# Hybrid encoder layer on eight cores: the PSUM banks of the mixer's score pairs and of its other TensorE work put into one pool of five

## The chip, the cores and the metric

The kernel runs on the 8 cores of one Trainium2 chip. Every core takes one sequence of the batch of 8 (2048 tokens by 1024 features) through the whole layer; the cores exchange nothing. The metric is the device time of the slowest core, in microseconds (us). TensorE (PE) multiplies, ScalarE (ACT) and VectorE (DVE) take results out of PSUM, GpSimd (POOL) computes small columns and issues the weight loads, SyncE (SP) issues the other transfers. PSUM has 8 banks, numbered 0 to 7 here, each 128 partitions by 512 fp32.

## The reference

```python
mod = (jax.nn.silu(c) @ w_ada[l] + b_ada[l]).reshape(bsz, N_MOD, D_MODEL)
x = sandwich(x, swiglu FFN 1,  ..., 0.5)      # D_FF = 2816
x = sandwich(x, hybrid_mixer,  ..., 1.0)
x = sandwich(x, swiglu FFN 2,  ..., 0.5)
def sandwich(x, y_fn, g_pre, g_post, shift, scale, gate, weight):
    h = rms_norm(x, g_pre) * (1.0 + scale[:, None, :]) + shift[:, None, :]
    y = rms_norm(y_fn(h), g_post)
    return x + weight * gate[:, None, :] * y
def hybrid_mixer(...):                        # chunks of 64 tokens
    proj = h @ w_in + b_in                    # qa ka va qb kb vb, 2304 columns
    oa = band attention, 8 heads on 2 kv heads, own + 2 chunks back, ALiBi, sinks
    ob = band attention, 8 heads, own + 8 chunks back, relative-position bias
    return concat(rms_norm(oa), rms_norm(ob)) @ w_out + b_out
```

The attention of both groups is a plain softmax over a band of keys: scores, exponential, product with V, division by the sum. All weights are used in bf16, sums are fp32.

## The kernel before

A core works its sequence in two halves of 1024 tokens, each of 8 tiles of 128 tokens (`m` = 0 to 7). For each half the program runs gate/up of the first FFN (lines 635 and 638), its down product (666 and 676), the mixer, gate/up of the second FFN and its down product. In the second half the mixer's first tiles also see keys of the first half, so that it has 56 score pairs against 45 in the first.

Every instruction is recorded by `S.op` into the queue of one engine, with the keys that it reads and writes; a PSUM bank is one such key. At run time each engine takes its queue in strict order, and an instruction waits until the keys that it needs are free. The order of the queues is decided while the program is built. The recorder also keeps a small model of time (`S.t`, `S.avail`, the `cost` arguments), and the mixer's main loop asks it, each time round, which of the candidate pieces of PE work could start first.

The pieces of PE work of a mixer are these. In the rows of the order and of the profile each is known by its lines.

- **Score pair** (`s_pair`, lines 878 with 882 or 888): scores of one key tile for two sets of four heads, into two banks. The bias is put in first by a product with the identity (878). Then ACT takes both banks out as two exponentials into `PT` (line 894). At most 8 units (4 pairs) may be pending ahead of their products with V.
- **PV unit** (`pv_unit`, line 916, 4 small matmuls): one exponential times V, summed in banks 2, 3 and 4. Two belong to a pair.
- **Fillers**: projections of the half's second four tiles (`proj_T` line 711, 13 pieces; `proj_VA` line 740 and `proj_V` line 725, four each), and 40 pieces of gate/up of the second FFN (`gu_chunk` line 787). Gate/up pieces may start only when the tail of tile 3 is done, since they read the new HT of tiles 0 to 3. A gate piece is taken out by ACT (Tanh, 793) and then DVE (795), an up piece by DVE (799).
- **Tail of a tile**, a chain of 13 steps across the engines: group norm of the attention's result (ACT 943, POOL 484 and 486, DVE 955), transposes (PE 966, DVE 970), output projection in two halves of 8+1 matmuls (PE 981 and 983), square and gate of each half (ACT 574, DVE 580), the residual (DVE 592), the next norm (ACT 495, DVE 502), and transposes into HT (`back2`, PE 524, ACT 509 and DVE 512).

Before the change the banks are in three groups. Score pairs rotate over banks 0, 1 and 5. PV sums live in 2, 3 and 4. Everything else, fillers and tails, uses 6 and 7:

```python
SBANKS = (0, 1, 5)
sb_ = [SBANKS[(u + r) % 3] for r in range(2)]
cbanks = [6, 7]
```

Output half `hh` always takes bank 6 + hh, and while it waits for its gate the bank is in the set `hold`, so that no filler takes it; with both held no filler is a candidate. The last transposes of a tail take 6 and 7 together. When all score pairs and PV units are recorded (`late`), fillers get banks 0 to 5 instead. The weight loads are recorded when a filler has released its ring slot, one megabyte each, three slots, in a fixed order.

Of the kernel before, what the change touches and what calls it, by code (L numbers as in the profile page):

```python
# [164 lines left out]
def build_nc(stage=3, dbg=False):  # L165
# [96 lines left out]
    S = Sched()  # L262
# [253 lines left out]
    def back(s, t, xb, bank, split=True):  # L516
        src, skeys = XBUF[xb]
        where = lambda k: (bank + 1, (k - 4) * 128) if split and k >= 4 else (bank, k * 128)
# [8 lines left out]
        S.op('pe', fn, reads=skeys + [("identb",)], writes=[ps_key(bank)] + ([ps_key(bank + 1)] if split else []), cost=0.46)  # L527
        for k in range(8):
            bk, c0 = where(k)
            mod_evac(s, k, HT[:, k, t * 128:(t + 1) * 128], PSB[:, bk, c0:c0 + 128], ps_key(bk),  # L530
                     [("HT", t, k)], bk != bank)
# [153 lines left out]
    def mixer(hf):  # L685
# [91 lines left out]
        cbanks = [6, 7]  # L777

# [59 lines left out]
        SBANKS = (0, 1, 5)  # L838
# [13 lines left out]

        def s_deps(u):
# [3 lines left out]
            return kk[0 if kind == "A" else 1] + qk, [ps_key(SBANKS[(u + r) % 3]) for r in range(2)]  # L857
# [10 lines left out]
        def s_pair(u):  # L868
# [4 lines left out]
            sb_ = [SBANKS[(u + r) % 3] for r in range(2)]  # L873
# [102 lines left out]
        def tail_b(m, hh):  # L976
            hold.add(6 + hh)

            def fn2(e):
                for k in range(8):  # L980
                    e.matmul(PS[6 + hh][:], lhsT=HT[:, k, m * 128:(m + 1) * 128], rhs=WOUT[:, hh, k, :],  # L981
                             start=(k == 0), stop=False)
                return e.matmul(PS[6 + hh][:], lhsT=ONES[:, :], rhs=BHL[:, 640 + hh * 512:640 + (hh + 1) * 512],
                                start=False, stop=True)
            S.op('pe', fn2, reads=[("wo", hh)] + [("HT", m, k) for k in range(8)] + [("ones",), ("bhi",), ("blo",)],
                 writes=[ps_key(6 + hh)], regions=("R1hi",), cost=1.94)

        def back2(m):
            back(2, m, m % 2, 6)

        chains = {}
        hold = set()
# [3 lines left out]

        def first_free(banks):
            return min(banks, key=lambda b: S.avail('pe', [], [ps_key(b)]))

        def chain(m):  # L1000
# [4 lines left out]
            bb = [ps_key(6), ps_key(7)]  # L1005
            ta = lambda: first_free([b for b in (6, 7) if b not in hold])

            def sq(hh):
                if hh == 0:
                    v["c"] = newst(2)  # L1010
                half_square(6 + hh, v["c"] + hh)
                if hh == 1:
                    v["p"] = None

            def gate(hh):
                half_gate(m, hh, 6 + hh, v["c"] + hh)
                hold.discard(6 + hh)
                if hh == 1:
                    v["p"] = half_root(v["c"])

            def fsq():
                v["f"] = front_square(X[:, m, :], fx)
            chains[m] = [
                ('act', lambda: (xh, [("sg", 0)]), lambda: o_norm(m, v), ()),
                ('dve', lambda: (stk(), [("yb", 0), ("yb", 1)]), lambda: o_scale(m, v), ()),
                ('pe', lambda: ([("yb", 0), ("yb", 1)], [ps_key(ta())]), lambda: tail_a(m, ta()), None),
                ('pe', lambda: ([("HT", m, 0)], bb[0:1]), lambda: tail_b(m, 0), (6,)),
                ('pe', lambda: ([("HT", m, 0)], bb[1:2]), lambda: tail_b(m, 1), (7,)),
                ('act', lambda: (bb[0:1], [("sg", 0)]), lambda: sq(0), ()),
                ('dve', lambda: (bb[0:1] + [("st", v["c"])], xh), lambda: gate(0), ()),  # L1030
                ('act', lambda: (bb[1:2], [("sg", 0)]), lambda: sq(1), ()),
                ('dve', lambda: (bb[1:2] + [("st", v["c"] + 1)], xh), lambda: gate(1), ()),
                ('dve', lambda: ([("st", v["p"])] + xh, fx), lambda: post_add(m, False, hf, v["p"]), ()),
                ('act', lambda: (fx, [("sg", 0)]), fsq, ()),
                ('dve', lambda: ([("st", v["f"])], xh), lambda: front_scale(X[:, m, :], fx, m % 2, v["f"]), ()),
                ('pe', lambda: (xh, bb), lambda: back2(m), (6, 7))]
# [312 lines left out]
```

## Time and profile before

| | |
|---|---|
| three runs | 1364.27, 1365.14, 1462.91 us, median 1365.14 |
| the profiled execution | 1369.62 us, of which 1367.7 us lie between its first and last instruction |
| spans of the 8 cores | 1358.3 to 1367.7 us, the profiled one is the longest |
| PE busy | 1285.5 us, 94% of the span |
| ACT, DVE, POOL busy | 447.7, 457.3, 188.1 us |
| scheduled part of the mixer, first half | about 336 to 543 us |
| scheduled part of the mixer, second half | about 972 to 1199 us |

A busy time says how long an engine had an instruction at work. What is left of a window is idle, and for PE that is what this document is about. The granted clock is a share of TensorE's full speed: 1.00 is the level of 2.4 GHz, and a window that was partly at 1.2 GHz has a figure between. A row of the timeline has the start, the duration, the engine, the line, what is written from what, and in brackets the idle time before it with what ended it.

### The profile page before, as it was taken

How to read it: one execution, taken by the hardware profiler on the slowest of the kernel's cores; microseconds unless marked ns; L12 is line 12 of the kernel's file. 1: busy time of each engine (PE TensorE's matmuls, PEld its weight loads, DVE VectorE, ACT ScalarE, POOL GpSimd, SP SyncE). 2: the span in 40 equal slices, each digit the busy share in tenths (PEclk: the TensorE clock that was granted, in tenths of full speed). 3: DMA queues.
4: the chain of work that ended last, by engine and by line, in shares of the span. 5: the costliest groups of instructions: out<-in, count | busy, mean ns of one | idle time of the engine just before them, and what ended most of it. 6: DMA issues, size and time to landing. Idle time of an engine off the chain costs nothing.

```text
span 1367.7 us, 21754 instructions; the slowest of 8 cores (1358.3 to 1367.7 us)
## 1 busy us (share of the span) xinstructions
PE 1285.5 (94%) x7941; PEld 611.2 (45%) x7941; DVE 457.3 (33%) x835; ACT 447.7 (33%) x902; POOL 188.1 (14%) x394
## 2 busy tenths in 40 slices
PE   2799999999989999999999999999998799999997
PEld 1344444554444444444444444444444344444443
DVE  2131122452454454222442122243143445522122
ACT  2241111342656552212341111233465655221110
POOL 3011101120121112101220000111011111200000
PEclk9999999999999999999999999999999999999999
DMA  9998977658243339993558756203542034899111
GB/s 174 173 201 144 169 130 125 113 88 158 47 85 73 69 69 163 169 156 122 170 144 156 126 101 113 38 0 65 91 84 41 2 63 92 146 162 159 43 47 61
DMA packets 32095, 148.24 MB, mean 108 GB/s; under 512 B 3274, under 2 KB 8567, under 8 KB 20344
## 3 DMA queue, kind: packets, MB, share of 16 engines
q0 software_dynamic: 26128, 129.64, 54.1%
q1 hardware_dynamic: 5864, 17.22, 3.5%
q8 instruction: 65, 1.06, 0.3%
q14 instruction: 38, 0.31, 0.1%
HBM read 258.36 MB, written 8.40 MB: 195 GB/s over the span
## 4 chain that ended last, share of the span: by engine, by line
PE 87%; DMA 4%; ACT 3%; DVE 2%; issue 2%; POOL 0%; DVEq 0%; ACTq 0%; POOLq 0%
PE psall L676 21%; PE psall L635 17%; PE psall L638 17%; PE psall L787 10%; PE psall L711 6%; PE psall L981 4%; DMA RING<-w_gu 3%; PE psall L878 3%; PE psall L725 2%; PE psall L916 2%; PE psall L888 1%; PE psall L666 1%; DMA R<-w_ada 1%; PE psall L524 1%; ACT R L894 1%
## 5 line engine op out<-in xcount | busy, mean ns | idle before, releaser
L676 PE MATMUL psall<-R 128*128 128x512 bf16 x1320 | 288.7, 379 | 0.0
L635 PE MATMUL psall<-HT,RING 128*128 128x512 bf16 x928 | 221.5, 382 | 6.0 <-DMA RING<-w_gu 4.9
L645 DVE TENSOR_TENSOR R<-SG,psall 128x512 bf16<-128x512 f32 x136 | 93.4, 687 | 381.3 <-ACT SG L643 357.7
L638 PE MATMUL psall<-HT,RING 128*128 128x512 bf16 x928 | 220.5, 381 | 0.0
L643 ACT ACTIVATE SG<-psall 128x512 f32<-128x512 f32 x136 | 81.2, 597 | 375.9 <-PE psall L638 375.7
L676 PEld LDWEIGHTS psall<-R 128*128 128x128 bf16 x1320 | 128.4, 98 | 151.2
L787 PE MATMUL psall<-HT,RING 128*128 128x512 bf16 x640 | 151.1, 387 | 4.2 <-ACT HT L509 2.4
L635 PEld LDWEIGHTS psall<-HT,RING 128*128 128x128 bf16 x928 | 90.7, 98 | 115.9 <-issue 10.8
L638 PEld LDWEIGHTS psall<-HT,RING 128*128 128x128 bf16 x928 | 91.2, 98 | 110.7 <-issue 3.1
L894 ACT ACTIVATE R<-psall 128x512 bf16<-128x512 f32 x202 | 109.7, 597 | 66.9 <-PE psall L888 50.9
L711 PE MATMUL psall<-HT,RING 128*128 128x512 bf16 x416 | 95.2, 380 | 0.2 <-ACT HT L509 0.2
L560 ACT ACTIVATE SG<-psall 128x1024 bf16<-128x1024 f32 x32 | 32.8, 1024 | 188.7 <-PE psall L676 188.7
L787 PEld LDWEIGHTS psall<-HT,RING 128*128 128x128 bf16 x640 | 60.0, 99 | 75.0 <-issue 18.9
L484 POOL TENSOR_SCALAR ST<-ST 128x1 f32<-128x1 f32 (+1 forms) x108 | 26.3, 244 | 419.8 <-ACT SG L560 184.2
L568 DVE TENSOR_TENSOR XH<-psall,GG 128x1024 f32<-128x1024 f32 x32 | 39.1, 1222 | 133.3 <-ACT SG L560 133.3
L509 ACT ACTIVATE HT<-psall,COLA,GMOD 128x128 bf16<-128x128 bf16 (+1 forms) x180 | 68.7, 464 | 23.3 <-DVE COLA L442 15.3
L285 POOL DMA_DIRECT2D RING<-w_gu x53 | 30.9, 586 | 317.7 <-PE psall L638 225.5
L486 POOL TENSOR_TENSOR ST<-ST,NHALF 128x1 f32<-128x1 f32 (+1 forms) x108 | 69.3, 641 | 16.7 <-POOL ST L484 1.3
L592 DVE SCALAR_TENSOR_TENSOR X<-XH,ST,X 128x1024 f32<-128x1024 f32 x48 | 61.6, 1284 | 10.5 <-DVE XH L568 5.1
L981 PE MATMUL psall<-R,HT 128*128 128x512 bf16 x256 | 61.0, 381 | 0.4 <-DVE HT L970 0.4
L711 PEld LDWEIGHTS psall<-HT,RING 128*128 128x128 bf16 x416 | 38.5, 98 | 45.6 <-issue 2.6
L495 ACT ACTIVATE SG<-X 128x1024 bf16<-128x1024 f32 x40 | 42.2, 1056 | 50.4 <-DVE X L592 48.6
(131 smaller groups left out, 1062.8 us busy)
## 6 DMA issues: line engine op xcount, KB each, us to landing
RING<-w_gu POOLq DMA_DIRECT2D x53, 1024.0 KB, 9.8
R<-w_down POOLq DMA_DIRECT2D x44, 512.0 KB, 17.3
R<-w_ada POOLq DMA_DIRECT2D x10, 1024.0 KB, 20.5
RING<-w_in POOLq DMA_DIRECT2D x10, 1024.0 KB, 9.9
RING<-w_ada POOLq DMA_DIRECT2D x8, 1024.0 KB, 9.8
out<-X SPq DMA_DIRECT2D x16, 512.0 KB, 2.6
R<-w_gu POOLq DMA_DIRECT2D x5, 1024.0 KB, 54.0
X<-x POOLq DMA_DIRECT2D x8, 512.0 KB, 27.2
```

The lines of the kernel that those rows point to most:

```text
L486: S.op('pool', lambda e: e.tensor_tensor(out=ST[:, c3:c3 + n], in0=ST[:, c3:c3 + n], in1=NHALF[:, 0:n], op=ALU.pow), reads=k1 + [("nhalf", ...
L509: S.op('act', lambda e: e.activation(out=dst, in_=psrc, func=AF.Identity, bias=sh, scale=GMOD[:, s, k:k + 1]), reads=rd, writes=wkeys, cos ...
L592: S.op('dve', lambda e: e.scalar_tensor_tensor(out=X[:, t, :], in0=XH[:, xb, :], scalar=ST[:, c3:c3 + 1], in1=X[:, t, :], op0=ALU.mult, op ...
L635: e.matmul(PS[bG][:], lhsT=rb[:, k, jj * 128:(jj + 1) * 128], rhs=HT[:, k, tb * 512:(tb + 1) * 512], start=(k == 0), stop=(k == 7))
L638: ins = e.matmul(PS[bU][:], lhsT=rb[:, k, 256 + jj * 128:256 + (jj + 1) * 128], rhs=HT[:, k, tb * 512:(tb + 1) * 512], start=(k == 0), sto ...
L643: S.op('act', (lambda e, bG=bG, sgi=sgi: e.activation(out=SG[:, sgi, :], in_=PS[bG][:], func=AF.Silu)), reads=[ps_key(bG)], writes=[("sg", ...
L645: S.op('dve', (lambda e, bU=bU, sgi=sgi, j=j, tb=tb: e.tensor_tensor(out=AT[:, tb, j, :], in0=SG[:, sgi, :], in1=PS[bU][:], op=ALU.mult)), ...
L676: ins = e.matmul(PS[bk][:], lhsT=AT[:, t // 4, j, (t % 4) * 128:(t % 4 + 1) * 128], rhs=WD[:, j, hh * 512:(hh + 1) * 512], start=(j == 0), ...
L711: ins = e.matmul(PS[bank][:], lhsT=RING[:, slot, k, g * 128:(g + 1) * 128], rhs=HT[:, k, tb * 512:(tb + 1) * 512], start=(k == 0), stop=(k ...
L787: ins = e.matmul(PS[bank][:], lhsT=RING[:, slot, k, part * 256 + jj * 128:part * 256 + (jj + 1) * 128], rhs=HT[:, k, 0:512], start=(k == 0 ...
L894: S.op('act', (lambda e, r=r, pi=pi: e.activation(out=PT[pi], in_=PS[sb_[r]][:], func=AF.Exp, scale=0.125)), reads=[banks[r]], writes=[("p ...
L981: e.matmul(PS[6 + hh][:], lhsT=HT[:, k, m * 128:(m + 1) * 128], rhs=WOUT[:, hh, k, :], start=(k == 0), stop=False)
```

## The change

`SBANKS` and `cbanks` go. There is one list, `pool = [0, 1, 5, 6, 7]`. A score pair takes the two banks of the pool that the model of time says are free first and that are not in `hold`. A filler, the first transposes of a tail and each output half take the one that is free first; an output half keeps the bank that it got in `v["b", hh]` until its gate is recorded. The last transposes take the two free first. A step that needs a bank for an output half is not a candidate while two banks are held, but fillers no longer stop then. When `late` comes, banks 2, 3 and 4 join the pool (in all 8 banks against 6 before). No instruction is added or taken away; the order and the banks are new.

```diff
-        SBANKS = (0, 1, 5)
+        pool = [0, 1, 5, 6, 7]
+        hold = set()
+        def two_free():
+            return sorted([b for b in pool if b not in hold], key=lambda b: S.avail('pe', [], [ps_key(b)]))[:2]
+        def first_free():
+            return two_free()[0]
...
-            return kk[0 if kind == "A" else 1] + qk, [ps_key(SBANKS[(u + r) % 3]) for r in range(2)]
+            return kk[0 if kind == "A" else 1] + qk, [ps_key(b) for b in two_free()]
...
-        def tail_b(m, hh):
-            hold.add(6 + hh)
+        def tail_b(m, hh, bank):
+            hold.add(bank)
...
-            back(2, m, m % 2, 6)
+            back(2, m, m % 2, two_free())
...
-            if len(hold) == 2 if need is None else any(b in hold for b in need):
+            if len(hold) >= 2 and need:
                 return False
...
-            fn(first_free(free_banks()))
+            fn(first_free())
...
-                cbanks[:] = [0, 1, 5, 2, 3, 4]
+                pool[:] = [0, 1, 5, 2, 3, 4, 6, 7]
```

The rows below are in the order in which PE takes them, equal rows merged with a count. 128x512 x2 of the identity is the start of a score pair, 128x65 are PV units of four matmuls each. The changed file has its lines about seven further down: 878 is 885 there, 882 is 889, 888 is 895, 916 is 923, 711 is 712, 725 is 726, 740 is 741, 787 is 786, 966 is 973, 981 is 988, 524 is 525.

**Place 1.** PE at the start of the first half's scheduled part, before:

```order
L878 MATMUL psall<-EA,IDENTB 128x512 x2
L882 MATMUL psall<-R 128x512 x2
L711 MATMUL psall<-HT,RING 128x512 x8
L916 MATMUL psall<-R 128x65 x8
L878 MATMUL psall<-EB,IDENTB 128x512 x2
L888 MATMUL psall<-R 128x128 x8
L711 MATMUL psall<-HT,RING 128x512 x8
```

and with the change:

```order
L885 MATMUL psall<-EA,IDENTB 128x512 x2
L889 MATMUL psall<-R 128x512 x2
L885 MATMUL psall<-EB,IDENTB 128x512 x2
L895 MATMUL psall<-R 128x128 x8
L712 MATMUL psall<-HT,RING 128x512 x8
L923 MATMUL psall<-R 128x65 x16
```

A filler stood after every pair; now it stands after every second, and the PV units follow two pairs behind their scores.

**Place 2.** PE in the second half, from the last projection piece to the first gate/up piece, where only pairs and tails are left. Before, there are 16 pairs in it, of which the first two stand here:

```order
L725 MATMUL psall<-RING,HT 128x512 x8
L727 MATMUL psall<-BHL,ONES 128x512
L916 MATMUL psall<-R 128x65 x8
L878 MATMUL psall<-EA,IDENTB 128x512 x2
L882 MATMUL psall<-R 128x512 x2
L916 MATMUL psall<-R 128x65 x4
L524 MATMUL psall<-IDENTB,XH 128x128 x8
L916 MATMUL psall<-R 128x65 x4
L878 MATMUL psall<-EB,IDENTB 128x512 x2
L888 MATMUL psall<-R,KBP 128x128 x8
L916 MATMUL psall<-VBP,R 128x65 x4
L966 MATMUL psall<-IDENTB,YB 128x128 x8
```

and with the change there are 9, of which the first two stand here:

```order
L726 MATMUL psall<-RING,HT 128x512 x8
L728 MATMUL psall<-BHL,ONES 128x512
L988 MATMUL psall<-R,HT 128x512 x8
L990 MATMUL psall<-BHL,ONES 128x512
L988 MATMUL psall<-R,HT 128x512 x8
L990 MATMUL psall<-BHL,ONES 128x512
L923 MATMUL psall<-R 128x65 x8
L885 MATMUL psall<-EB,IDENTB 128x512 x2
L895 MATMUL psall<-R 128x128 x8
L885 MATMUL psall<-EB,IDENTB 128x512 x2
L895 MATMUL psall<-R 128x128 x8
L923 MATMUL psall<-R 128x65 x4
```

The last projection piece stood behind pair 22 of the half's 56; now it stands behind pair 32. The first gate/up piece stood behind pair 38; now it stands behind pair 41.

**Place 3.** PE in the first half, where the four small projections (740) meet the output projection of a tile, before:

```order
L981 MATMUL psall<-R,HT 128x512 x8
L983 MATMUL psall<-BHL,ONES 128x512
L916 MATMUL psall<-R 128x65 x12
L740 MATMUL psall<-RING,HT 128x128 x8
L742 MATMUL psall<-BHL,ONES 128x128
L740 MATMUL psall<-RING,HT 128x128 x8
L742 MATMUL psall<-BHL,ONES 128x128
L740 MATMUL psall<-RING,HT 128x128 x8
```

and with the change:

```order
L988 MATMUL psall<-R,HT 128x512 x8
L990 MATMUL psall<-BHL,ONES 128x512
L923 MATMUL psall<-R 128x65 x16
L712 MATMUL psall<-HT,RING 128x512 x32
L741 MATMUL psall<-RING,HT 128x128 x8
L743 MATMUL psall<-BHL,ONES 128x128
L741 MATMUL psall<-RING,HT 128x128 x8
```

Four large projections (712) now stand between the output projection and the small ones.

## Rows read from the trace of the kernel before

**Rows 1.** The page: busy times of the engines, and the chain that ended last by engine.

```profile
PE 1285.5 (94%) x7941; PEld 611.2 (45%) x7941; DVE 457.3 (33%) x835; ACT 447.7 (33%) x902; POOL 188.1 (14%) x394
...
PE 87%; DMA 4%; ACT 3%; DVE 2%; issue 2%; POOL 0%; DVEq 0%; ACTq 0%; POOLq 0%
```

**Rows 2.** Windows of core 7: length, busy of PE, PEld, DVE, ACT, POOL, clock, DMA.

```profile
336.00:543.00 207.00, 197.81 (x1491) 94.73 (x1489) 101.25 (x209) 109.39 (x234) 34.25 (x76) 0.97 0.47 83
400.00:410.00 10.00, 9.46 (x47) 4.49 (x47) 3.84 (x8) 3.41 (x6) 2.43 (x5) 0.73 0.56 106
972.00:1199.00 227.00, 209.91 (x1680) 101.68 (x1680) 101.47 (x210) 120.51 (x256) 34.18 (x76) 0.98 0.39 69
1040.00:1086.00 46.00, 33.22 (x338) 16.84 (x337) 20.29 (x49) 30.73 (x71) 8.12 (x19) 0.93 0.13 24
1040.00:1050.00 10.00, 7.29 (x68) 4.05 (x67) 4.59 (x12) 6.46 (x16) 2.71 (x5) 0.68 0.56 105
```

**Rows 3.** Groups of instructions by line, PE, 1040 to 1086 us.

```profile
L878 PE MATMUL psall<-EB,IDENTB 128*128 128x512 bf16 x22 | 7.4, 423 | 0.0
...
L878 PE MATMUL psall<-EA,IDENTB 128*128 128x512 bf16 x10 | 3.0, 379 | 0.0
```

**Rows 4.** Groups of instructions by line, ACT, 1040 to 1086 us.

```profile
L894 ACT ACTIVATE R<-psall 128x512 bf16<-128x512 f32 x32 | 17.3, 596 | 8.5 <-PE psall L888 6.7 <-PE psall L882 1.7
```

**Rows 5.** Waits of PE, 1040 to 1086 us: total, times, longest.

```profile
PE psall L916 <- ACT R L894: 8.9, 10, 1.9
PE psall L787 <- ACT HT L509: 1.6, 1, 1.6
```

**Rows 6.** Timeline of PE, pairs without a filler.

```profile
1075.02 0.40 PE L888 MATMUL psall<-R 64*128 64x128 bf16 x8
1076.26 0.28 PE L916 MATMUL psall<-R 128*128 128x65 bf16 x4 [0.84 <-ACT R L894]
1076.38 0.59 PE L878 MATMUL psall<-EB,IDENTB 128*128 128x512 bf16 x2
...
1077.23 0.30 PE L916 MATMUL psall<-R 128*128 128x65 bf16 x4
```

**Rows 7.** Timeline of ACT, the same place.

```profile
1075.52 1.08 ACT L894 ACTIVATE R<-psall 128x512 bf16<-128x512 f32 x2 [0.27 <-PE psall L888]
1077.40 1.08 ACT L894 ACTIVATE R<-psall 128x512 bf16<-128x512 f32 x2 [0.80 <-PE psall L888]
1078.37 1.06 ACT L495 ACTIVATE SG<-X 128x1024 bf16<-128x1024 f32 x1
```

**Rows 8.** Waits of PE, 336 to 543 us.

```profile
PE psall L740 <- DVE XH L580: 2.6, 1, 2.6
PE psall L916 <- ACT R L894: 2.5, 9, 0.4
PE psall L878 <- ACT R L696: 1.0, 1, 1.0
```

**Rows 9.** Timeline of PE, first half, around the small projections.

```profile
398.98 1.01 PE L740 MATMUL psall<-RING,HT 128*128 128x128 bf16 x8 [2.58 <-DVE XH L580]
...
401.55 3.62 PE L725 MATMUL psall<-RING,HT 128*128 128x512 bf16 x8
...
406.69 1.90 PE L725 MATMUL psall<-RING,HT 128*128 128x512 bf16 x8
```

**Rows 10.** Timeline of DVE, the two gates that free the banks of one tile.

```profile
394.61 0.69 DVE L580 TENSOR_TENSOR XH<-psall,GG 128x512 f32<-128x512 f32 x1 [3.27 <-ACT SG L574]
...
398.15 0.68 DVE L580 TENSOR_TENSOR XH<-psall,GG 128x512 f32<-128x512 f32 x1
```

**Rows 11.** Timeline of all engines, a gate piece and what takes it out.

```profile
1090.62 1.89 PE L787 MATMUL psall<-HT,RING 128*128 128x512 bf16 x8
...
1092.61 0.60 ACT L793 ACTIVATE SG<-psall 128x512 f32<-128x512 f32 x1 [1.19 <-PE psall L787]
1093.37 0.69 DVE L795 SCALAR_TENSOR_TENSOR SG<-SG,psall 128x512 f32<-128x512 f32 x1 [1.26 <-ACT SG L793]
```

## What the change will do: the prediction

> **What bounds the kernel now.** I read the busy times first. PE is at work for 1285.5 of 1367.7 us, and 87% of the chain that ended last is PE's own work [rows 1]. The other engines are busy for a third of the span. So PE is the bound, no PE instruction is taken away, and the change can win only what PE idles, or runs at the low clock, inside the two scheduled parts of the mixer. Outside of them nothing is edited.
>
> Then I read the windows of these two parts [rows 2]. In the first half PE is busy 197.81 of 207 us, so it idles 9.2. In the second it is busy 209.91 of 227, so it idles 17.1. Together 26.3 us, 1.9% of the time. Of the 17.1 us, 46 - 33.22 = 12.8 lie in one stretch, 1040 to 1086 us. That stretch is the one where all projections are used up and the gate/up pieces are not allowed yet. The reader is to see there 32 products with the identity [rows 3], so 16 pairs, 2.9 us each, and 32 exponentials [rows 4].
>
> Why PE idles there is in the waits: 8.9 us in ten waits of PV units for ACT's exponentials, and 1.6 us for the first gate/up piece, which waits for the HT of tile 3 [rows 5]. But ACT is not full either, 30.73 of 46 us [rows 2]. The timelines show the loop. A pair's last score products end at 1075.42; the two exponentials run from 1075.52; the first PV unit starts at 1076.26, after 0.84 us idle, and the next pair right behind it at 1076.38 [rows 6]. Its exponentials start at 1077.40, and ACT idled 0.80 us before them [rows 7]. Each engine waits for the other: with three banks, of which a pair takes two, the next pair needs a bank of the pair before. The period is 77.40 - 75.52 = 1.88 us, of which ACT has 1.08 for two exponentials.
>
> **The thin stretch, with the change (Places 1 and 2).** It acts twice. Five banks let a second pair stand between PE and ACT, so the loop opens: in Place 2 two pairs stand back to back and PV units follow a pair or two behind. And since pairs run ahead where fillers are, fillers last longer: 9 pairs are left uncovered and not 16.
>
> What would the nine cost? PE's own work in the stretch is 33.22 us for 16 pairs with their tails, 2.08 a pair, ACT's is 30.73 / 16 = 1.92 a pair [rows 2]. So even when the loop is open the two engines are nearly level, and a little idle time must stay. Low end: none but the 1.6 us for HT, which is a true dependence on tile 3. High end: the same idle rate as before, 12.8 x 9/16 = 7.2 us. I take 4, nearer to the low end, since the loop of rows 6 and 7 is what the extra banks break. **Gain 8.8 us** (5.6 to 11.2).
>
> **The rest of the second half.** 17.1 - 12.8 = 4.3 us of idle time in 181 us, in single waits of under a microsecond or so. The one at the start, a score pair that waits for the evacuation of a projection (the first half has the same, 1.0 us [rows 8]), stays: the first banks taken are again 0 and 1. **Gain 2 us** (0 to 3.3).
>
> **The first half.** 9.2 us idle. One wait is 2.6 us [rows 8]: a small projection needs bank 7, which holds an output half until DVE has gated it. DVE's queue had the division of the next tile between the two gates of this one, so that the second ran 3.5 us after the first, from 398.15 to 398.83 [rows 10], and PE went on at 398.98 [rows 9]. With the change this projection takes any free bank of three, and four large projections stand ahead of it (Place 3). It goes. Another 2.5 us are nine waits of PV units for exponentials [rows 8], of which the deeper queue takes most. 1.0 us at the start stays. The other 3.1 us are single waits on HT and on gates. I take 2.6 + 2.0 + 0.9 = 5.5. **Gain 5.5 us** (2.6, the one wait alone, to 8.2, all but the start).
>
> **The clock.** Behind both stretches the granted clock falls: 0.73 from 400 to 410 us and 0.68 from 1040 to 1050 [rows 2]. Before the first fall stood the 2.6 us wait; the second fell while PE idled for exponentials. The price is in the durations: the projection at 401.55 took 3.62 us against 1.90 for the same one at 406.69 [rows 9], 1.7 us. Of the 1.01 us of the small one at 398.98, at the same ratio, 0.5 is the clock's, and its neighbour's is alike, so the first fall cost about 2.5 us; the second, of like depth and length, is taken as 2.4. They need not go with their waits, and new ones may come. **Gain 2.5 us**, half of the 4.9 (0 to 4.9).
>
> The Trainium skill (TensorE: Matmul & The Clock Gate, "Why this matters for your kernels") says that idle gaps between bursts of matmuls bring TensorE back to its lower clock. By it both falls would go with the gaps, and this term would be the whole 4.9. The trace agrees that both falls lie in idle stretches. But the whole stretch has 0.93 in the mean and its first ten us 0.68, so the other 36 us ran at (46 x 0.93 - 6.8) / 36 = 1.00 although PE idled in them as well [rows 2]. Idle time and clock don't go together closely, and I keep the half.
>
> **What is added.** No instruction, transfer or byte. POOL's queue keeps its loads in the same ring order. Seven fewer pairs behind the last projection means that the loads released by projections are issued later in the half, yet nine pairs and an output projection, over 20 us, still stand between the last projection and the first gate/up piece; I cost the loads at nothing. The cover is that distance; without it a late load would show as a wait of line 786 on the ring. What is added is **coupling**: a score pair can now be given a bank whose last user was a gate/up piece, and behind a waiting pair stand all of PE's queue and ACT's exponentials. A gate piece that ended on PE at 1092.51 was taken by ACT at 1092.61 and by DVE from 1093.37 to 1094.06 [rows 11], so its bank is free 1.6 us after its end, and an exponential's bank 0.7 to 1.2 us after the pair's [rows 6, 7]. In the new order three banks are used per cycle of a pair, two PV units and a filler, about 3 us, so a bank comes back after 5/3 of a cycle, 5 us. That covers it where the model of time is right. Where it is wrong, PE waits. Below: 0. Above: a wait of 0.8 us, like that of rows 6, in every seventh of the about 85 cycles with a filler (61 fillers a half less the 19 or so behind the last pair, twice), 10 us. **Cost 4 us**, nearer the low end because the 5 us are three times the 1.6.
>
> **Sum.** 8.8 + 2 + 5.5 + 2.5 - 4 = 14.8 us. The profiled execution had 1369.6, so 1354.8. The median of the runs, 1365.1, is 4.5 us under that execution, so the forecast is **1350 us**, 1.1% faster. Of this kernel a change of under 2%, 27 us, can't be told from none here.
>
> **Rivals.**
>
> *The banks were not the limit.* PE and ACT are level in the thin stretch (2.08 against 1.92 us a pair), so breaking the loop could give nothing there: PE then waits for ACT in longer pieces. For it: the tails put another 13 us of ACT work between the exponentials (30.73 - 17.3) [rows 2, 4], and a pair's exponentials can stand behind them; only moving seven pairs under cover is left, and the new waits eat that. Against it: ACT idled 0.80 us before a pair that was next in its queue [rows 7]. Gain then the 2.6 us wait and about 1 more: 1361.5 us. Chance 0.23. In the Trainium skill (TensorE: Matmul & The Clock Gate, "HAM oscillation") double-buffering PSUM gave a kernel no further gain once its loop was in order; by that the time would be this rival's, or none at all.
>
> *All the waits go.* Idle 26.3 less 1.0 at each start and 1.6 for HT is 22.7, and 4.9 of clock: 27.6 us, 1337.5 at the edge of 2%. For it: nothing but loops and banks stands in the waits of rows 5 and 8. Against it: near level engines. Chance of 1342 or less 0.09, of more than 2% 0.03.
>
> *Slower, by coupled banks.* The mechanism of the last term, not rare but regular: in the stretches with gate/up pieces every pair meets a bank whose gate piece still waits behind a tail's work in DVE's queue. One division kept the second gate 3.5 us behind the first [rows 10]. Before, only fillers met that. If in each of the 85 cycles a pair waited 0.6 us, it would cost 51 us against 18.8 gained, 1397 us. It decides from 18.8 / 85 = 0.22 us a cycle upward, and is over 2% from 0.54. Against it: the 5 us of distance, three times the release. Chance of slower at all 0.07, of over 2% slower 0.02.
>
> **Chances and range.** Forecast (1342 to 1358) 0.61; banks not the limit (1358 to 1366) 0.23; all the waits 0.09; slower 0.07. The range 1341 to 1364 leaves out about 0.07 below and 0.12 above. Faster by over 2%: 0.03; within 2%: 0.94; slower: 0.03.
>
> **What would show it.** In the second half the stretch between the last projection and the first gate/up piece should be under 25 us with 18 exponentials, ACT over 80% busy in it, and PE's waits of PV units for exponentials 3 us or less over the half, against 8.9 in the stretch alone. In the first half the wait of the small projection on DVE's gate should be gone, and the total idle time of the first part about 4 us, of the second about 7. Coupling would show as waits of score pairs (now line 885) on DVE's or ACT's evacuation of gate/up pieces, above 4 us together. I would be wrong if the first gate/up piece waits long for HT, because tile 3's tail, now behind more exponentials in ACT's queue, ends later than the pairs run out, or if a clock fall moves into the projections.

## The result, and the profile after

| | before | after |
|---|---|---|
| median of the runs, us | 1364.99 | 1339.32 |
| profiled execution, us | 1369.62 | 1339.02 |
| its longest span, us | 1367.7 | 1337.5 |

The ratio of the times is 0.9816, with an interval of 0.9803 to 0.9829. The change makes the kernel 1.8% faster, 25.7 us: inside the 2% bound, but clear of no change by its interval. The forecast was 1350 us in a range of 1341 to 1364, so the gain was larger than forecast and the time lies just under the range. A later comparison gave 0.9827 (0.9814 to 0.984). Some executions, of most kernels here, are longer at a lower clock on the four cores of one die or on all eight (1591.43 us once, of the changed kernel); the ratios and intervals leave them out, the medians don't.

In the profiled executions the cores 0 to 3 had mean clocks of 0.989 to 0.998, and their median span is 1360.9 us before and 1334.7 us after, 26.2 us less. So the gain doesn't rest on cores 4 to 7, whose clock was lower in the profile before (0.987 to 0.990).

First the page of the changed kernel: the span, the busy times, and the chain that ended last by engine.

```profile
span 1337.5 us, 21760 instructions; the slowest of 8 cores (1332.2 to 1337.5 us)
...
PE 1272.5 (95%) x7941; PEld 606.3 (45%) x7941; DVE 456.9 (34%) x835; ACT 445.2 (33%) x902; POOL 188.0 (14%) x394
...
PE 91%; DMA 4%; ACT 1%; issue 1%; DVE 1%; POOL 0%; DVEq 0%; ACTq 0%; another core or an unknown queue 0%; POOLq 0%
```

PE is busy for 13.0 us less than before with the same 7941 matmuls [rows 1]. So the gain is not idle time alone. The rows that follow are those of core 0, the slowest, where no other core is named. The windows of the two scheduled parts, which now end earlier, and of the thin stretch in the second half (columns as in rows 2):

```profile
332.00:532.00 200.00, 195.96 (x1512) 94.90 (x1510) 103.57 (x213) 109.13 (x235) 34.32 (x76) 1.00 0.49 89
960.00:1169.00 209.00, 203.48 (x1680) 99.33 (x1680) 101.99 (x211) 119.51 (x256) 34.22 (x76) 1.00 0.42 75
1044.00:1062.00 18.00, 15.86 (x185) 8.06 (x183) 7.88 (x20) 13.99 (x32) 3.30 (x8) 1.00 0.31 60
```

PE idles 4.0 us in the first part (9.2 before) and 5.5 in the second (17.1 before). The clock is 1.00 in all three windows, where it was 0.97, 0.98 and 0.93 [rows 2]. The thin stretch has 9 pairs in 18 us, 2.0 a pair, against 16 in 46 us, 2.9 a pair. PE is at work for 88% of it and ACT for 78% (the prediction had said over 80%). From the first output projection at 1044.28 to the first gate/up piece at 1061.61 it is 17.3 us, under the 25 of the prediction. PE's waits (total, times, longest), in the first half,

```profile
PE psall L885 <- ACT R L697: 1.0, 1, 1.0
PE psall L636 <- DVE R L798: 0.9, 1, 0.9
...
PE psall L923 <- ACT R L901: 0.6, 2, 0.3
```

and in the second:

```profile
PE psall L525 <- ACT R L901: 1.6, 1, 1.6
PE psall L885 <- ACT R L697: 1.0, 1, 1.0
PE psall L636 <- DVE R L798: 0.9, 1, 0.9
...
PE psall L923 <- ACT R L901: 0.3, 1, 0.3
```

The ten waits of PV units for exponentials in the thin stretch, 8.9 us [rows 5], are gone; of this kind 0.3 us is left. So is the 2.6 us wait of the small projection for a gate [rows 8]. No score pair waits for the evacuation of a gate/up piece, on any core. The 1.0 us in each half at line 885 is the first pair, as before. The one wait that answers to the coupling that the prediction feared is the 1.6 us of line 525. Behind the last pair of a half the pool has eight banks, six before; PE idles 1.2 us there before and 1.6 after, so these two banks are no part of the gain.

One sign that the prediction had named did show, on some cores: gate/up pieces that wait for their weights. Core 4 of the same execution:

```profile
PE psall L786 <- DMA RING<-w_gu: 1.4, 1, 1.4
```

Cores 2 and 7 have 0.4 and 0.9 us of it, and in the later profile of the same kernel four cores have 0.4 to 1.7 us. Before, no core has such a wait in the two parts.

The timeline of PE in the thin stretch, core 0 again, shows the wait of line 525 and the open loop:

```profile
1051.16 0.42 PE L923 MATMUL psall<-R 128*128 128x65 bf16 x8
1051.41 0.59 PE L885 MATMUL psall<-EA,IDENTB 128*128 128x512 bf16 x2
1051.94 0.39 PE L889 MATMUL psall<-R 64*128 64x512 bf16 x2
1052.26 0.42 PE L923 MATMUL psall<-R 128*128 128x65 bf16 x8
1052.52 0.59 PE L885 MATMUL psall<-EA,IDENTB 128*128 128x512 bf16 x2
...
1058.18 0.61 PE L525 MATMUL psall<-IDENTB,XH 128*128 128x128 bf16 x8 [1.55 <-ACT R L901]
```

From one pair (1051.41) to the next (1052.52) it is 1.11 us, against 1.88 in rows 6 and 7, and eight PV matmuls stand between without a wait. At 1058.18 the last transposes of tile 3 had to wait for a bank whose exponential stood in ACT's queue. ACT in the same place:

```profile
1049.44 3.04 ACT L901 ACTIVATE R<-psall 128x512 bf16<-128x512 f32 x6 [0.27 <-PE psall L895]
...
1053.36 2.10 ACT L901 ACTIVATE R<-psall 128x512 bf16<-128x512 f32 x4
...
1057.35 2.04 ACT L901 ACTIVATE R<-psall 128x512 bf16<-128x512 f32 x4
```

Six exponentials run back to back in 3.04 us, where ACT idled 0.80 us before a pair of them [rows 7]. The exponential for which line 525 waited is the first at 1057.35; it had the two group norms of the next tile (950, not shown, 1055.85 to 1057.45) ahead of it in ACT's queue.

I timed the stages on all cores from the timelines. A half is counted from the first `proj_V` to the first gate/up product behind the mixer; what lies between the halves is 398.6 us in both kernels and behind the second half 168.4 us.

| core of the profiled execution | first half, us (PE busy) | second half, us (PE busy) |
|---|---|---|
| before, core 7 (the slowest) | 236.0 (226.3) | 257.2 (239.0) |
| before, core 1 (fewest clock falls) | 233.3 (223.1) | 253.6 (234.3) |
| after, core 0 (the slowest) | 224.3 (220.1) | 238.4 (232.6) |
| after, core 1 | 224.1 (219.9) | 238.4 (232.6) |

Of core 7's 30.5 us, 9.7 + 18.2 - 4.2 - 5.8 = 17.9 are idle time and 12.6 are busy time. The busy part has three sources. The falls behind waits, at 400 and 1040 us, are in rows 2. Further falls stood in dense stretches late in the parts, on cores 4 to 7 alone; on core 7 they come to about 4.5 us, an estimate from the clocks of its 5 us windows. These are windows of core 7 and of core 1 of the kernel before, the same stretch, each counted from its core's own start:

```profile
515.00:525.00 10.00, 10.00 (x49) 4.66 (x48) 6.04 (x9) 1.20 (x2) 2.65 (x5) 0.89 1.04 172
```

```profile
515.00:525.00 10.00, 10.00 (x54) 4.81 (x53) 4.07 (x6) 1.54 (x4) 0.00 (x0) 1.00 1.01 163
```

PE was at work all the time on both, and only core 7 was at 0.89. And third, the end of a matmul's row is hidden only if another matmul follows at once. The four PV matmuls at 1076.26 have a row of 0.28 us, but the next row starts 0.12 us after them [rows 6]; ahead of a wait the whole row counts as busy. Core 1 has 49 places where PE ran out of work in the two halves before, and 20 after. It had one fall in the halves, of about 1.7 us by the windows, and has 4.9 us less busy time after. The other 3.2 us are put down to these row ends, 0.11 us for each of the 29 places; that is what is left over, and no run tests it. The profile models the ends of matmuls, so where busy time stops and idle time starts is its choice; the sum of both is not.

### The profile page after: what moved, and what is told of

Read it like the earlier page. It is cut to its first block, busy times and chain, and to the rows that moved or that the text cites. A ratio compares the mean times of both kernels' runs of the same rounds, so it can differ in the third digit from the quotient of the medians.

```text
span 1337.5 us, 21760 instructions; the slowest of 8 cores (1332.2 to 1337.5 us)
## 1 busy us (share of the span) xinstructions
PE 1272.5 (95%) x7941; PEld 606.3 (45%) x7941; DVE 456.9 (34%) x835; ACT 445.2 (33%) x902; POOL 188.0 (14%) x394
## 4 chain that ended last, share of the span: by engine, by line
PE 91%; DMA 4%; ACT 1%; issue 1%; DVE 1%; POOL 0%; DVEq 0%; ACTq 0%; another core or an unknown queue 0%; POOLq 0%
PE psall L677 21%; PE psall L636 17%; PE psall L639 17%; PE psall L786 10%; PE psall L712 6%; PE psall L988 4%; PE psall L885 3%; DMA RING<-w_gu 3%; PE psall L726 2%; PE psall L923 2%; PE psall L895 2%; PE psall L667 1%; DMA R<-w_ada 1%; PE psall L525 1%; PE psall L437 1%
## 5 line engine op out<-in xcount | busy, mean ns | idle before, releaser
L639 PE MATMUL psall<-HT,RING 128*128 128x512 bf16 x928 | 219.9, 380 | 0.0
L901 ACT ACTIVATE R<-psall 128x512 bf16<-128x512 f32 x202 | 107.1, 599 | 44.1 <-PE psall L895 30.6
L509 ACT ACTIVATE HT<-psall,COLA,GMOD 128x128 bf16<-128x128 bf16 (+1 forms) x180 | 68.7, 464 | 24.4 <-DVE COLA L442 15.7
```

Source lines behind the costliest of these rows:

```text
L509: S.op('act', lambda e: e.activation(out=dst, in_=psrc, func=AF.Identity, bias=sh, scale=GMOD[:, s, k:k + 1]), reads=rd, writes=wkeys, cos ...
L639: ins = e.matmul(PS[bU][:], lhsT=rb[:, k, 256 + jj * 128:256 + (jj + 1) * 128], rhs=HT[:, k, tb * 512:(tb + 1) * 512], start=(k == 0), sto ...
L901: S.op('act', (lambda e, r=r, pi=pi: e.activation(out=PT[pi], in_=PS[sb_[r]][:], func=AF.Exp, scale=0.125)), reads=[banks[r]], writes=[("p ...
```

## The experiments

All times below are medians unless said otherwise, all ratios are to the kernel before as run on the same chip beside it. Waits and timelines are of the slowest core of the profiled execution unless a core is named. Every kernel has line numbers of its own.

**Banks alone.** The decisions of the kernel before were written down (`SCRIPT`), and the changed kernel was made to follow them. In the traces of both, the instructions stand in the same order on PE, ACT, DVE and POOL.

```diff
+            want = script.pop(0)
+            go = [c for c in cand if c[3] == want][0]
-            now = S.t['pe'] + 0.1
-            go = min(cand, key=lambda c: (max(c[0], now), c[1]))
```

> Every engine's queue stands in the order of the kernel before, instruction by instruction; only the banks are those that the pool of five gives. Theory A (order and banks are worth something only together: in the old order a PV unit stands right behind the scores it needs, so a free bank doesn't help): only the 2.6 us wait of the small projection for a gate goes, with its clock fall, 2 to 6 us gained, about 1360 us; the waits of PV units for exponentials in the second half stay above 8 us. Theory B (the number of banks was the limit, the order only follows): most of the gain is here, 15 us or more, under 1350 us. Theory C (as in the prediction: the pool couples score pairs to slow evacuations): slower than the kernel before by up to 4 us.

Measured: 1362.27 us, ratio 0.9968 (0.9958 to 0.9978), 4 us of the 25. Waits of PE in the second half, and then in the first (926 is the PV unit, 904 the exponential, 976 the first transposes of a tail):

```profile
PE psall L926 <- ACT R L904: 11.7, 16, 1.9
```

```profile
PE psall L976 <- DVE YB L965: 3.0, 1, 3.0
PE psall L926 <- ACT R L904: 2.8, 10, 0.4
```

The waits for exponentials are all there (10.9 us in the same part of the kernel before). The small projection's wait is gone, but on this core a tail's first transposes wait 3.0 us in its place. Theory A holds in its time and in the waits that stay, but the clock fall near 400 us did not go: it is there on six of eight cores. Theories B and C fall: free banks with the old order win little, and they cost nothing. On core 1 the halves are 4.0 and 1.4 us shorter than before, 3.6 of it idle time.

**Order alone.** The order of the changed kernel (again the same on all four engines in the traces), the old groups of banks.

```diff
-            return sorted([b for b in pool if b not in hold], key=...)[:2]
+            return best([0, 1, 5])[:2]
...
-            return two_free()[0]
+            return best([b for b in (cbanks if late[0] else (6, 7)) if b not in hold] or [0, 1, 5])[0]
```

> Every engine's queue stands in the order of the changed kernel, but the banks are in the old groups: score pairs take two of 0, 1 and 5, everything else 6 and 7 (or, where both are held, one of 0, 1, 5). Theory A: two pairs back to back now need four banks and have three, so PE waits for exponentials at the second pair, about 0.9 us at each of some 30 such places; the gain of the fillers that are saved is eaten, 1350 to 1375 us. Theory D (saving fillers for the thin stretch is the whole gain): 1345 us or less. Theory B: no gain, 1365.

Measured: 1416.55 us, ratio 1.0376 (1.0358 to 1.0393). All three theories fell short here, A in size: the order without the banks loses 50 us. PE's waits, and the place where two pairs stand back to back (894 starts a pair, 910 is the exponential, 528 the last transposes of a tail, 801 what takes out an up piece):

```profile
PE psall L894 <- ACT R L910: 31.4, 32, 2.5
...
PE psall L528 <- DVE R L801: 6.5, 3, 3.1
```

```profile
348.83 0.60 PE L894 MATMUL psall<-EB,IDENTB 128*128 128x512 bf16 x2
349.36 0.40 PE L904 MATMUL psall<-R 64*128 64x128 bf16 x8
351.34 0.59 PE L894 MATMUL psall<-EB,IDENTB 128*128 128x512 bf16 x2 [1.58 <-ACT R L910]
```

The second pair waits 1.58 us for the exponentials of the first, since four banks are wanted and three are there. Such waits are 31.4 us; fillers and tails, which have two banks, wait as well. So the two halves of the change are worth -4 us and +50 us one by one, and -25 us together.

**Only the pairs get the pool.**

```diff
-            return ..., [ps_key(SBANKS[(u + r) % 3]) for r in range(2)]
+            return ..., [ps_key(b) for b in two_free()]      # of 0, 1, 5, 6, 7
```

> The kernel before, but score pairs may take any two of the five banks that are not held; fillers and tails stay on 6 and 7 and stop while both are held. 36 of the second half's 56 pairs stand ahead of the first gate/up piece with 1 pair in the thin stretch (16 before, 9 with the change). Theory A and D (running ahead saves fillers): nearly all of the gain, 1338 to 1346 us. Theory E (the freedom of fillers and tails matters as much, above all while output halves hold both banks): less than half of it, 1352 us or more.

Measured: 1390.89 us, ratio 1.018 (1.0163 to 1.0197), 24 us slower. I had expected nearly the whole gain. The pairs take banks 6 and 7, and fillers, which may use no other, starve: in the first half only 4 of the 13 large projections are placed before tile 3's pairs are done, and 9 stand in one lump, as tile 4 can't start without them. Waits of PE, and the timeline ahead of and in the lump (711, with a tail's transposes and output projection between):

```profile
PE psall L787 <- DMA RING<-w_gu: 10.2, 2, 5.6
...
PE psall L524 <- DVE XH L502: 6.4, 1, 6.4
```

```profile
390.33 0.61 PE L524 MATMUL psall<-IDENTB,XH 128*128 128x128 bf16 x8 [1.38 <-DVE XH L580]
392.29 5.30 PE L711 MATMUL psall<-HT,RING 128*128 128x512 bf16 x16 [1.36 <-DVE ST L933]
398.52 8.79 PE L711 MATMUL psall<-HT,RING 128*128 128x512 bf16 x39 [0.93 <-ACT R L696]
```

Pairs run uncovered, the tail's transposes wait up to 6.4 us for a norm, the lump's pieces wait for each other's evacuation on two banks, and the gate/up weights, whose loads wait for the projections to release the ring, are late by 10.2 us. The count of uncovered pairs between the last projection and the first gate/up piece (1 here) was a bad measure: the same hole had moved ahead of the lump.

**Only the fillers get the pool.**

```diff
-        cbanks = [6, 7]
+        cbanks = [0, 1, 5, 6, 7]
```

> The kernel before, but fillers may take any of the five banks; score pairs rotate over 0, 1, 5, tails stay on 6 and 7. Fillers go earlier: the last projection stands behind pair 13 in either half, with 14 and 25 pairs in the thin stretches (2 and 16 before). Theories A and D: slower, by 0.8 us for each of the 21 more uncovered pairs, 17 us, 1375 to 1390 us. Theory E: faster than before.

Measured: 1423.84 us, ratio 1.0421 (1.0404 to 1.0438). Theory E falls. The direction of A and D was right, the size over three times what 0.8 us a pair gives:

```profile
PE psall L916 <- ACT R L894: 20.2, 26, 2.0
PE psall L524 <- DVE XH L502: 16.3, 5, 7.1
PE psall L635 <- DMA RING<-w_gu: 13.9, 3, 5.0
```

Waits for exponentials are up from 13.4 us before, but the larger part is in waits that the estimate did not have, for norms, and for weights at the gate/up phase (13.9 us with the 5 of every run).

**Fixed banks for the tails.** Pairs and fillers share the five; a tail keeps 6 and 7.

```diff
-                v["b", hh] = first_free()
+                v["b", hh] = 6 + hh
...
-            back(2, m, m % 2, two_free())
+            back(2, m, m % 2, 6)
```

> The changed kernel, but a tail keeps banks 6 and 7 for its output halves and its last transposes, and one of them for its first transposes; pairs and fillers use all five. 13 pairs are uncovered in the second half (9 in the changed kernel). Theory L (pairs and fillers sharing a pool is what matters): within 5 us of the changed kernel, under 1345 us. Theory M (a tail that waits for just one bank, while pairs and fillers keep taking it, comes late, and with it the release of tile 3's HT and of the gate/up pieces): 10 us or more slower than the changed kernel, 1350 us or more, with waits of line 525 and 988.

Measured: 1351.06 us, ratio 0.9886 (0.9873 to 0.99), 8 us slower than the changed kernel in the same comparison (1342.91). Between the theories, nearer to M; waits of PE:

```profile
PE psall L786 <- DMA RING<-w_gu: 3.9, 1, 3.9
PE psall L525 <- DVE XH L581: 3.9, 2, 2.2
```

The last transposes wait 3.9 us for a gate on their fixed bank, and the gate/up pieces 3.9 us for weights. It is still 15.5 us faster than the kernel before beside it (1366.58), so pairs and fillers in one pool bring most of the gain, and the tails in it the rest.

**How deep a lead?** First at most two pairs ahead of their PV, then none.

```diff
-            if u < NU and len(pend) <= NPT - 2 and not blocked:
+            if u < NU and len(pend) <= 2 and not blocked:      # and, in the second, <= 0
```

> The changed kernel, but a score pair is a candidate only while at most one pair (two units) waits for its PV (four pairs before), so the lead of scores over PV is at most two pairs. Theory F (the loop is open as soon as one more pair stands between PE and ACT): within 4 us of the changed kernel, 1338 to 1343 us, ratio to the kernel before 0.980 to 0.984. Theory G (the deep lead matters, since it saves fillers and bridges ACT's tail work): a third or more of the gain is lost, 1348 us or more.

Measured: 1341.27 us, ratio 0.9829 (0.9812 to 0.9847), the same as the changed kernel's within the intervals. Theory F holds.

> The changed kernel, but a score pair is a candidate only when no PV unit waits, so that PE alternates between the scores of a pair and its own PV; 13 and 22 pairs are uncovered (1 and 9 in the changed kernel). Five banks are free to use. Theory F and G: the loop between PE and ACT is closed again and the thin stretch is longer than in the kernel before, about 1 us idle for each of 35 pairs, 1375 to 1395 us. Theory B (banks are the limit, the lead is not): within 5 us of the changed kernel.

Measured: 1381.75 us, ratio 1.0126 (1.011 to 1.0142). Waits of PE:

```profile
PE psall L923 <- ACT R L901: 19.5, 36, 1.0
```

With five banks and no lead the waits for exponentials are back, 36 of them. The lead is what the banks buy, and one pair more of it is enough. This kernel also leaves more pairs uncovered (22 against 9), so it doesn't part the lead from the fillers that it saves.

**Who chooses the bank?** The pool taken in turn.

```diff
+        turn = [0]
-            return sorted([b for b in pool if b not in hold], key=...)[:2]
+            return [b for b in pool[turn[0]:] + pool[:turn[0]] if b not in hold][:2]
+        def took(b):
+            turn[0] = (pool.index(b) + 1) % len(pool)
```

> The changed kernel, but the pool of five is taken in turn (held banks skipped) and not by the scheduler's choice of the bank free first. 5 pairs are uncovered in the second half. Theory H (coupling is harmless because five uses lie between two of one bank, whoever chooses): within 4 us of the changed kernel, 1337 to 1344 us. Theory I (the choice is what avoids the coupling: in turn, a score pair or a tail's transposes meet a bank whose evacuation is still queued on DVE): 8 us or more slower than the changed kernel, 1348 us or more, in waits of score pairs and transposes for DVE's and ACT's evacuation.

Measured: ratio 0.9897 (0.9845 to 0.9949). It is made of 1345.38, 1347.65 and 1357.96 us, and in the last the mean clock of cores 0 to 3 was 0.986 to 0.989. The other two are 4 to 6 us above the 1341.27 us of the kernel with a lead of two pairs, on the same chip. In the profiled execution the halves of core 1 took 227.4 and 243.0 us, 3.3 and 4.6 more than after; 3.8 of these 7.9 us are idle time and 1.7 a clock fall behind a wait. Waits of PE on core 2, the slowest (929 is the PV unit, 907 the exponential):

```profile
PE psall L929 <- ACT R L907: 2.3, 8, 0.7
PE psall L929 <- DVE ST L943: 2.1, 4, 0.8
...
PE psall L786 <- DVE HT L512: 1.9, 3, 0.8
PE psall L891 <- DVE XH L581: 1.5, 3, 0.9
```

Pairs (891) now do wait for DVE's gates of output halves, 1.5 us, and gate/up pieces for the bank of transposes that DVE takes out, 1.9 us. So coupling appears when nobody chooses, though no pair waits for a gate/up piece here either. Theory I has the mechanism, but its 8 us or more is not shown: the two times without the low clock lie at the edge of theory H (1344) and below the 1348 of theory I.

**What a wait does to the clock.** Four gaps put into the changed kernel.

```diff
+        GAPS = [20, 34]
+        def idle():
+            for i in range(4):
+                S.op('pool', lambda e: e.tensor_tensor(out=GAPT[:], in0=EPSC[:], in1=NHALF[:, 0:1], op=ALU.pow),
+                     reads=last[:1] if i == 0 else (), writes=[("gap",)])
```

> The changed kernel in its own order, with four idle gaps put into PE: twice in each half (behind pairs of unit 20 and 34) the next PE instruction waits for four small dependent operations of POOL, 0.57 us each and about 0.15 us between them, that start when PE's last instruction is done; so each gap is 2.6 to 3 us long if POOL is free. Theory J (a gap of this length brings the clock down behind it, as at 398 us of the kernel before, where the fall cost 2.5 us): each gap costs its length and about 2 us more, 18 to 24 us in all, 1358 to 1363 us, with granted clocks of 0.5 to 0.9 in the windows behind the gaps. Theory K (falls came from something else): 10 to 13 us in all, 1350 to 1352 us, and the clock stays 1.00.

Measured: 1366.74 us, ratio 1.0029 (1.0003 to 1.0054), 25 us more than the kernel with a lead of two pairs on the same chip, and 28 by the ratios to the kernel before, of which this one takes in an execution of 1381.47 us with a clock of 0.81 outside the halves. The gaps were longer than planned, 19.1 us together (5.9 the longest, 2.9 the shortest), so 6 to 9 us are left. On core 6, where no such 0.81 stands, PE is busy 8.4 us longer in the halves than after, with four falls: about 2 us for each. Timeline of core 6 behind one gap, and its windows (930 is the PV unit, 719 a projection):

```profile
991.36 0.60 PE L930 MATMUL psall<-R 128*128 128x65 bf16 x8 [5.91 <-POOL GAPT L1115]
...
993.50 3.03 PE L719 MATMUL psall<-HT,RING 128*128 128x512 bf16 x8
...
996.49 1.89 PE L719 MATMUL psall<-HT,RING 128*128 128x512 bf16 x8
```

```profile
990.00:995.00 5.00, 3.64 (x26) 1.73 (x27) 0.00 (x0) 1.09 (x2) 1.07 (x2) 0.50 0.00 0
995.00:1000.00 5.00, 5.00 (x48) 2.66 (x47) 2.49 (x4) 0.69 (x1) 0.00 (x0) 0.92 0.00 0
```

The projection at 993.50 took 3.03 us against 1.89 for the next one, and the clock was 0.50, the level of 1.2 GHz, for the 5 us behind the gap. Behind the three gaps of 4.6, 5.7 and 5.9 us it fell on all eight cores, behind the one of 2.9 us on three. Theory J holds in its mechanism, and in its size of about 2 us a fall.

There was one more fall, on seven cores, and it stood behind no inserted gap but behind the changed kernel's own wait for a bank (line 525 after, 532 here). Core 6:

```profile
1080.09 0.61 PE L532 MATMUL psall<-IDENTB,XH 128*128 128x128 bf16 x8 [1.56 <-ACT R L908]
```

```profile
1080.00:1085.00 5.00, 4.89 (x57) 2.79 (x58) 1.89 (x6) 4.35 (x11) 0.60 (x1) 0.66 0.00 0
```

The same wait of 1.55 us brought no fall on any core in the first profile of the changed kernel, and one on one core of eight in the later profile. So the same short wait has a fall behind it in one execution and none in another; what decides it, these runs don't show.

**A version that beats both.** The two waits at the ends of each half.

```diff
-        pool = [0, 1, 5, 6, 7]
+        pool = [5, 6, 7, 1, 0]
...
+            avoid = {0, 1} if late[0] and len(lst) < 3 else set()
+            hold.update(avoid)
             fn(first_free())
+            hold.difference_update(avoid)
```

> The changed kernel itself once more, as the measure for the two that run with it on the same chip: 1339 us, ratio to the kernel before 0.980 to 0.983.

Measured: 1342.91 us, ratio 0.9827 (0.9814 to 0.984).

> The changed kernel in the same order on every engine, with two edits to its banks: the pool is listed as 5, 6, 7, 1, 0, so that the first pair of a half doesn't take banks 0 and 1, which the last projections ahead of it still hold; and the last three gate/up pieces leave banks 0 and 1 to the gate/up phase that follows. If a wait in PE's queue costs what its row says (1.0 and 0.9 us in each half), all four go: 3.8 us, 1335.5 us, ratio to the changed kernel 0.997. If another wait takes the place of each (a filler or a second pair on the banks that the first pair no longer takes): under 1.5 us, which can't be told from none.

Measured: 1339.03 us, ratio 0.9791 (0.9777 to 0.9804), 3.9 us under the changed kernel beside it; the intervals don't overlap. Waits of PE over the whole program:

```profile
PE psall L525 <- ACT R L901: 1.6, 1, 1.6
...
PE psall L636 <- ACT SG L644: 1.1, 1, 1.1
...
PE psall L885 <- ACT R L697: 0.4, 1, 0.4
```

Of line 885's 2.1 us 0.4 are left, and the gate/up phase waits once, 1.1 us, and not twice 0.9 for the evacuation of the last pieces. The queues of all four engines stand in the same order as in the changed kernel's trace. It is the fastest kernel here.

## Why the prediction was wrong

**The bound and the place** were right. PE bounds, the halves are the only stages that changed, and the thin stretch gave most.

**The thin stretch**, predicted 8.8 us of idle time (5.6 to 11.2): 12.8 before, 2.1 after, so 10.7. The loop opened and fillers were saved, as written. One reading was wrong: the prediction puts the loop down to the three banks, but in rows 6 it is a PV unit that waits 0.84 us for its exponential, and the next pair stands behind it in PE's queue. The order closes the loop too. That banks and order are needed together is shown by banks alone (4 us faster), order alone (50 us slower) and five banks without a lead (17 us slower). How much of the 10.7 us is the open loop, and how much the seven pairs now under cover, no run separates.

**The rest of the second half**, predicted 2: 5.4 before, 3.7 after, 1.7. **The first half**, predicted 5.5: 9.7 before, 4.2 after, 5.5. Both held.

**The clock**, predicted 2.5 us of 4.9. This is the first term that was mis-sized. Every fall in the halves went, on all eight cores of the profiled execution. (The 4.9 is itself low: the rows of the first fall add up to 1.7 + 0.5 + 0.5 = 2.7 us, not 2.5.) I had given half of them back because idle time and low clock did not match closely in the thin stretch; the gap experiment shows that falls do follow waits, about 2 us each. The Trainium skill (TensorE: Matmul & The Clock Gate, "Why this matters for your kernels") says that idle gaps between bursts of matmuls bring the lower clock back. The traces agree: both falls of core 7 stood behind waits and went with them. That all went has some luck in it, since in the later profile of the same kernel two of the eight cores had one fall each in the second half.

**What the sum had no term for.** About 3.2 us of busy time that went are put down above to row ends ahead of waits; my sum was made of idle time and clock alone. And the profiled execution before lost about 4.5 us in dense stretches, which I had not looked for. The forecast had taken this off unseen, as the 4.5 us between that execution and the median.

**What is added**, the coupling, predicted 4 us of cost. This is the second term that was mis-sized, and the larger one. Nothing of it came but the 1.6 us wait of line 525, and that already stands in the idle time after. The prediction's own argument, 5 us between two uses of a bank against 1.6 until it is free, spoke for no cost, and I charged for it all the same; the 5 us themselves were not measured. Taking the banks in turn cost 4 to 6 us in all, not all of it coupling. The loads, which I had put at nothing, cost something on some cores: 0.4 to 1.7 us of waits of line 786.

On the profiled executions the change gave 30.6 us and not 14.8. The 15.8 us between are idle time 1.6 (17.9 against 16.3), the clock behind waits 2.4, the coupling 4.0, the row ends 3.2 and the dense stretches 4.5, which add up to 15.7. With the first sum, the two terms put right and the row ends added, 8.8 + 2 + 5.5 + 4.9 + 3.2 - 0 = 24.4 us, 1340.7 at the median.

Core 1, which had one fall in the halves before, gained 9.2 + 15.2 = 24.4 us too, but as 19.5 idle, 3.2 row ends and 1.7 clock. That the two sums are equal is chance.

**The rivals.** The time is that of "all the waits go" (chance 0.09, 1342 or less), but its mechanism did not come: it left 3.6 of the 26.3 us idle, and 9.5 stayed. The row ends, which no rival had, made up for half of this, so its number is partly luck. "The banks were not the limit" is refuted, in that the lead needs them, and partly right in that banks alone give only 4 us. "Slower, by coupled banks" did not come in the changed kernel. With turn-taking, waits of its kind appear, but for gates and transposes and not for gate/up pieces.

Not settled: why cores 4 to 7 of the kernel before ran at about 0.9 in dense stretches, whether the change has any part in its absence afterwards, and when a short wait has a clock fall behind it.

## What to carry to other kernels

Look at banks and order together. Here more banks helped only as far as the queue's order used them for a lead, and the order with a lead needed its banks. Where a scheduler chooses the banks, try one pool for everything that shares the engine: here a larger pool for one side starved the other or used up its cover. And a wait on TensorE cost more here than its idle row: about 0.1 us by the end of the last matmul ahead of it (an estimate from core 1, 3.2 us over 29 places) and, where the clock fell behind it, about 2 us more.

## What the runs showed that I had not expected

- A pool for one side alone is worse than none: 24 us slower with pairs alone, 58 with fillers alone. With both it is 15.5 us faster, and with the tails too about 25.
- A lead of up to two pairs is worth as much as one of up to five (ratios 0.9829 and 0.9816, intervals overlapping).
- The clock was 0.89 on one core and 1.00 on another in the same 10 us of their spans, both with PE at work for the whole window.
- The same wait of 1.55 us had a clock fall behind it on no core of eight in one execution and on seven in another.
